# A hybrid decoder step on one core: five buffers for the decay rows, and the convolution half of the output projection ahead of the scan's half

## What is computed

```python
proj = rmsnorm(h) @ w_in                        # 1024 -> gate/value of a conv, z, x/B/C, dt
glu   = proj[:, :1024] * sigmoid(proj[:, 1024:2048])
a_out = silu(layernorm(causal_dwconv(glu)))     # 31 taps, 1024 channels: the "conv half"
xbc   = silu(causal_dwconv(proj[..., o2:o3]))   # 4 taps
y     = ssd_scan(x, dt, a_neg, B, C, state)     # 16 heads in 4 groups, chunks of 128
y     = (y + d_skip * x) * silu(z)
m_out = rmsnorm(y per group of 256)             # the "state half"
h = h + concat(a_out, m_out) @ w_out            # 2048 -> 1024
h = h + hier_moe(rmsnorm(h))                    # 16 experts, 2 of a token's group
h = h + (p @ w_ple) * sigmoid(rmsnorm(h) @ w_ple_gate)
return rmsnorm(h), and the new conv and scan states
```

## Time and profile before

| what | value |
|---|---|
| time, median of 3 runs (lowest to highest) | 586.15 us (583.11 to 587.26) |
| profiled execution: its time, its span | 586.09 us, 584.4 us |
| mean granted TensorE clock | 0.98 |
| busy: PE, DVE, ACT, POOL | 540.7, 265.1, 164.1, 85.2 us |
| HBM read, written | 155.06 MB, 8.84 MB |

### The profile page before, as it was taken

How to read it: one execution, slowest core, us unless ns; L and a number is a source line. 1 busy time by engine, 2 the same in 40 slices (tenths; PEclk the granted TensorE clock), 3 DMA queues, 4 the chain that set the end, 5 groups by cost and what they waited for, 6 DMA issues and landing times.

```text
span 584.4 us, 7620 instructions
## 1 busy us (share of the span) xinstructions
PE 540.7 (93%) x2749; PEld 351.1 (60%) x2749; DVE 265.1 (45%) x783; ACT 164.1 (28%) x386; POOL 85.2 (15%) x103
## 2 busy tenths in 40 slices
PE   5999999997896878999989899999999999999994
PEld 3788888885555657888764334343434343444882
DVE  0799798438447776102253032323232322323653
ACT  3211311116568783502242111111101010102433
POOL 4000063413425540030000000000000000000000
PEclk9999999999989879999989999999999999999997
DMA  8844443687956867793296996999999999999001
GB/s 339 270 145 146 144 145 144 169 238 234 253 181 202 296 232 315 296 370 152 93 384 259 421 422 270 382 423 422 421 423 421 421 422 420 423 419 422 33 0 74
DMA packets 35692, 164.27 MB, mean 281 GB/s; under 512 B 5768, under 2 KB 12744, under 8 KB 19664
## 3 DMA queue, kind: packets, MB, share of 16 engines
q1 hardware_dynamic: 25200, 140.27, 62.1%
q0 software_dynamic: 5920, 21.27, 10.3%
q10 hardware_dynamic: 4544, 2.37, 1.5%
HBM read 155.06 MB, written 8.84 MB: 280 GB/s over the span
## 4 chain that ended last, share of the span: by engine, by line
PE 86%; DVE 7%; issue 2%; DMA 2%; ACT 1%; POOL 1%; DVEq 0%; POOLq 0%; ACTq 0%
PE ps L968 21%; PE ps L1220 19%; PE ps L1067 10%; PE ps L1250 10%; PE ps L1195 5%; PE ps L1283 5%; PE ps L917 2%; DMA asg<-acs_rows 2%; PE ps L1122 2%; DVE xraw_s L1502 1%; PE ps L1153 1%; PE ps L935 1%; PE ps L1147 1%; PE ps L1160 1%; PE ps L959 1%
## 5 line engine op out<-in xcount | busy, mean ns | idle before, releaser
L968 PE MATMUL ps<-u,ring 128*128 128x264 f32 x640 | 145.6, 389 | 0.0
L968 PEld LDWEIGHTS ps<-u,ring 128*128 128x128 f32 x640 | 122.6, 192 | 22.0 <-issue 0.8
L1220 PE MATMUL ps<-ring,xraw 128*64 128x512 f32 x464 | 103.0, 595 | 5.0 <-DVE glu L1714 4.9
L1220 PEld LDWEIGHTS ps<-ring,xraw 128*64 128x64 f32 x464 | 33.9, 137 | 62.6 <-issue 61.1
L1250 PE MATMUL ps<-ring,xraw 128*64 128x512 f32 x256 | 58.5, 598 | 0.7 <-ACT xraw L880 0.7
L1067 PE MATMUL ps<-cat,ring 128*128 128x264 f32 x256 | 57.6, 387 | 1.6 <-DVE cat L1552 1.6
L1067 PEld LDWEIGHTS ps<-cat,ring 128*128 128x128 f32 x256 | 48.5, 190 | 10.6 <-issue 2.4
L632 POOL DMA_INDIRECT xbc<-u_rows,slot_tok x8 | 7.6, 952 | 258.0 <-DVE slot_tok L1669 258.0
L1250 PEld LDWEIGHTS ps<-ring,xraw 128*64 128x64 f32 x256 | 16.9, 136 | 32.1 <-issue 28.8
L558 POOL TENSOR_TENSOR glu<-asg 128x256 f32<-128x256 f32 x8 | 21.4, 2673 | 96.3 <-ACT asg L704 96.3
L1714 DVE COPY glu<-ps 128x264 f32<-128x264 f32 x8 | 3.5, 433 | 68.2 <-PE ps L1260 68.2
(11 more groups left out here) (299 smaller groups left out, 631.8 us busy)
## 6 DMA issues: line engine op xcount, KB each, us to landing
ring<-in_w_moe SPq DMA_DIRECT2D x90, 1024.0 KB, 14.4
ring<-in_w_in SPq DMA_DIRECT2D x20, 1024.0 KB, 5.2
ring<-in_w_out SPq DMA_DIRECT2D x8, 1024.0 KB, 6.1
ring<-in_state_s POOLq DMA_DIRECT2D x8, 512.0 KB, 9.7
out_h_s_out<-ring POOLq DMA_DIRECT2D x8, 512.0 KB, 5.7
ring<-in_w_pleg SPq DMA_DIRECT2D x4, 1024.0 KB, 23.2
asg<-acs_rows ACTq DMA_DIRECT2D x8, 256.0 KB, 6.4
glu<-bc_rows POOLq DMA_DIRECT2D x4, 512.0 KB, 6.4
```

What stands on the lines that cost most here:

```text
L968: ins = mm(ps[:, BANK[n], 0:T], wv[:, k, q * P:(q + 1) * P], u[:, k, :], start=(k == 0), stop=(k == KD - 1))
L1220: ins = mm(ps[e * CAP:(e + 1) * CAP, gu, :], xg[:, 4 * hf + k, e * CAP:(e + 1) * CAP], wk, start=(hf == 0 and k == 0), stop=(hf == 1 and k ...
```

## The change

Two parts. First, `acs` gets five buffers instead of two (`NACS`): two where they were, three in `hs_all`, which is free once its rows have been turned; the three further spreads are issued right behind the first two, and later ones as buffers come free. Second, the order of the two halves of the output projection is exchanged. The layer norm's two means move into TensorE's scan loop (behind items 3 and 5), its subtraction, root, products and Silu into the loops of VectorE and ScalarE (items 4, 6 and 7). The conv half comes first, in banks 0, 1, 2 and 7, and VectorE adds its blocks to `h` one at a time (`add_a`); the state half follows and is added separately. ScalarE does the state `decode` of tiles 0 to 3 in the scan and of 4 to 7 behind it; VectorE does 0 to 2 in the scan. SP's table puts each `load_first` two weight loads later, and w_out's halves are taken in the other order.

```diff
-        acs = asg[:, :, :, :].rearrange("p a b n -> p (a b n)")[:, 0:8 * Q].rearrange("p (q r n) -> p q r n", q=2, r=4)
+        acs_of = lambda x, q: [x.rearrange("p a n -> p (a n)")[:, 4 * Q * i:4 * Q * i + 4 * Q].rearrange("p (r n) -> p r n", r=4)
+                               for i in range(q)]
+        acs = acs_of(asg[:, :, :, :].rearrange("p a b n -> p (a b) n"), 2) + acs_of(hs_all[:, :, :], 3)
+        AB = [0, 1, 2, 7]
 # SP
-                    sp.wait_ge(out_used, n - NWIN + 1)
+                    sp.wait_ge(a_psum, 2 * (n - NWIN) + 2)
-                src = w_in[n] if n < NWIN else w_out[n - NWIN]
+                src = w_in[n] if n < NWIN else w_out[(n - NWIN + NWOUT // 2) % NWOUT]
-                for j in {22: (0, 1, 2, 3), 23: (4, 5), 24: (6, 7), 25: (8,)}.get(n, ()):
+                for j in {24: (0, 1, 2, 3), 25: (4, 5), 26: (6, 7), 27: (8,)}.get(n, ()):
                     load_first(j)
 # GpSimd
-            pool.wait_ge(ln_n, 4)
 # ScalarE
             spread(0)
             spread(1)
+            act.wait_ge(htok_psum, 1)
+            for i in range(2, NACS):
+                spread(i)
...
+                if i == NG:
+                    act.wait_ge(ln_xc, 1)
+                    a.activation(ln_sqr, cat[:, 0:8, :], ACT.Square).then_inc(ln_sq, 1)
                 if i == 6:
+                    act.wait_ge(ln_stat, 2)
+                    link(a.activation(ps[:, 7, 0:T], ps[:, 7, 0:T], ACT.Ln, bias=eps[:, 0:1]))
+                    a.activation(ps[:, 7, 0:T], ps[:, 7, 0:T], ACT.Exp, scale=-0.5).then_inc(g_root, 1)
                     act.wait_ge(proj_evac, Z_SILU)
                     z0 = zs[:, 0:6, :]
                     a.activation(z0, z0, ACT.Silu)
-                decode(i)
+                if i == 7:
+                    for j in range(KD):
+                        act.wait_ge(ln_n, j // 2 + 1)
+                        a.activation(cat[:, j, :], cat[:, j, :], ACT.Silu, scale=par("ln_g", j), bias=par("ln_b", j))\
+                            .then_inc(a_out_ready, 1)
+                if i % 2:
+                    decode(i // 2)
...
             load_table(ACT.Ln)
+            decode(4)
+            decode(5)
+            square_y(0)
+            decode(6)
+            decode(7)
+            for gr in range(1, NG):
+                square_y(gr)
 # TensorE
                 item(i)
+                if i == 3:
+                    ...
+                    mean_of(cat, 7, mean_k).then_inc(ln_stat, 1)
+                if i == 5:
+                    pe.wait_ge(ln_sq, 1)
+                    mean_of(ln_sqr, 7, mean_k).then_inc(ln_stat, 1)
...
+            pe.wait_ge(proj_evac, NSEQ)
+            pe.wait_ge(xtok_ready, 4)
             for n in range(KD):
-                if n == KD - 1:
-                    pe.wait_ge(ln_n, 4)
-                w_out_half(n, 0)
-                if n == 2:
-                    pe.wait_ge(ln_sq, 1)
-                    mean_of(glu, 7, mean_k).then_inc(ln_stat, 1)
+                if n >= 4:
+                    pe.wait_ge(a_added, n - 3)
+                w_out_half(n, 0).then_inc(a_psum, 1)
+                if n == 3:
+                    pe.wait_ge(y_ready, 2 * NG)
+                    pe.wait_ge(st_ready, 2 * NG)
+                    pe.wait_ge(btok_ready, 2)
+                    group_mean(0)
+                if n == 6:
+                    for gr in range(1, NG):
+                        group_mean(gr)
 # VectorE
+                if i == NG:
+                    dve.wait_ge(ln_stat, 1)
+                    v.tensor_tensor(cat[:, 0:8, :], ...subtract).then_inc(ln_xc, 1)
                 take(i)
...
-                if i >= 2:
-                    decode(i - 2)
+                if i == 6:
+                    dve.wait_ge(g_root, 1)
+                    for j in range(0, KD, 2):
+                        v.tensor_tensor(cat[:, j:j + 2, :], ...mult).then_inc(ln_n, 1)
+                if i in (3, 5, 7):
+                    decode((i - 3) // 2)
...
+            def add_a(n):
+                dve.wait_ge(a_psum, n + 1)
+                v.tensor_tensor(h[:, n, :], h[:, n, :], ps[:, AB[n % 4], 0:T], ALU.add).then_inc(a_added, 1)
...
-            for gr in range(3):
-                gate_y(gr)
+            gate_y(0)
+            decode(3)
+            gate_y(1)
+            add_a(0)
+            decode(4)
+            add_a(1)
+            decode(5)
+            gate_y(2)
+            add_a(2)
             decode(6)
+            add_a(3)
             decode(7)
             gate_y(3)
```

More of the change, by code:

```diff
@@ L30 @@
 NPR = 256
+NACS = 5
 NSM = 8
@@ L131, in build @@
         x4 = scratch[:, 4096:6200].rearrange("p (q i t) -> p q i t", q=2, i=4)
-        outer = [scratch[:, at:at + 1024].rearrange("p (b n) -> p b n", b=NSM) for at in (8192, 9216, 6200)]
+        outer = [scratch[:, at:at + 1024].rearrange("p (b n) -> p b n", b=NSM) for at in (8192, 9216, 6208)]
+        ln_sqr = scratch[:, 4096:4096 + KD * T].rearrange("p (j n) -> p j n", j=KD)
         glu_s = scratch[:, 10240:12224].rearrange("p (j k b) -> p j k b", j=KD, k=KC)
@@ L286, in build @@
         rows_stored = sem("rows_stored")
-        acs_loaded = [sem(f"acs_loaded{q}") for q in range(2)]
+        acs_loaded = [sem(f"acs_loaded{q}") for q in range(2)] + in_x + [in_small]
+        NACS_BASE = [0, 0, 16, 16, 48]
         b_loaded = [sem(f"b_loaded{q}") for q in range(2)]
@@ L788, in _ @@
             exp_of(0)
-            spread(2)
             evacuate(NFIRST + 1)
@@ L802, in _, with square_y @@
                     a.activation(z0, z0, ACT.Silu)
-                decode(i)
+                if i == 7:
[5 more added lines that the diff above has]
+                    decode(i // 2)
                 for n in AFTER_ITEM[i]:
                     evacuate(n)
-            load_table(ACT.Ln)
-            for gr in range(NG):
+            def square_y(gr):
                 act.wait_ge(ycat_ready, gr + 1)
@@ L819, in _ @@
                 a.activation(o, o, ACT.Exp, scale=-0.5).then_inc(g_root, 1)
-            act.wait_ge(ln_xc, 1)
-            act.wait_ge(out_conf, 32)
-            a.activation(glu[:, :, 0:T], cat[:, 0:8, :], ACT.Square).then_inc(ln_sq, 1)
-            act.wait_ge(ln_stat, 2)
-            link(a.activation(ps[:, 7, 0:T], ps[:, 7, 0:T], ACT.Ln, bias=eps[:, 0:1]))
-            a.activation(ps[:, 7, 0:T], ps[:, 7, 0:T], ACT.Exp, scale=-0.5).then_inc(g_root, 1)
-            load_table(ACT.Silu)
-            for j in range(KD):
-                act.wait_ge(ln_n, j // 2 + 1)
-                a.activation(cat[:, j, :], cat[:, j, :], ACT.Silu, scale=par("ln_g", j), bias=par("ln_b", j))\
-                    .then_inc(a_out_ready, 1)
             load_table(ACT.Ln)
@@ L1041, in _, with group_mean @@
                 item(i)
+                if i == 3:
+                    pe.wait_ge(conv_done, KD - len(PE_CONV))
+                    pe.wait_ge(conv_s_done, 1)
+                    pe.wait_ge(proj_evac, POS["c", 7, 0] + 1)
+                    pe.wait_ge(btok_ready, 1)
+                    mean_of(cat, 7, mean_k).then_inc(ln_stat, 1)
+                if i == 5:
+                    pe.wait_ge(ln_sq, 1)
+                    mean_of(ln_sqr, 7, mean_k).then_inc(ln_stat, 1)
                 for n in AFTER_ITEM[i]:
                     project(n)
-            pe.wait_ge(conv_done, KD - len(PE_CONV))
-            pe.wait_ge(proj_evac, NSEQ)
-            pe.wait_ge(conv_s_done, 1)
-            pe.wait_ge(ea_ready, NG)
-            pe.wait_ge(dif_ready, 2 * NG)
-            mean_of(cat, 7, mean_k).then_inc(ln_stat, 1)
-            pe.wait_ge(rows_kept, 1)
-            pe.wait_ge(y_ready, 2 * NG)
-            pe.wait_ge(st_ready, 2 * NG)
-            for gr in range(NG):
+            def group_mean(gr):
                 pe.wait_ge(gsq_ready, gr + 1)
@@ L1553, in _ @@
                                            in1=ps[:, 3 + gr, 0:T], op0=ALU.mult, op1=ALU.mult).then_inc(m_out_ready, 1)
-            dve.wait_ge(g_root, NG + 1)
-            for j in range(0, KD, 2):
-                v.tensor_tensor(cat[:, j:j + 2, :], cat[:, j:j + 2, :],
-                                ps[:, 7, 0:T].unsqueeze(1).to_broadcast([P, 2, T]), ALU.mult).then_inc(ln_n, 1)
+            add_a(7)
+            dve.wait_ge(a_added, KD)
             def add_square(i, x, c):
```

48 lines of the change are left out of this document (27 added, 21 removed).

## The result

| | before | after |
|---|---|---|
| median (lowest to highest) | 584.98 us (581.04 to 587.26) | 589.26 us (586.44 to 592.44) |
| profiled execution: time, span | 586.09 us, 584.4 us | 590.0 us, 588.3 us |
| end of the output projection in it | 287.46 | 292.70 |

The medians are of 15 runs each, taken side by side. The ratio is 1.0068 (95% interval 1.0044 to 1.0093). The change is slower by 0.7%; 581.2 us had been predicted, within 575.5 to 588. The time lies above that range, and on the other side of the kernel before.

A forecast was written before the change was run, and what follows sets the result against it. TensorE was taken to bound the kernel (86% of the chain), but transfers to set the projection's new end: 287.5 - 282.6 = 4.9 us won, from 586.09 profiled (586.15 median) to 581.2 us, range 575.5 to 588.

The forecast's parts named there:

- The scan: TensorE's scan items: the second starts at 157.4, then 37.5 us back to back, so item seven ends at 194.9.
- ScalarE's chain: Between scan and projection, ScalarE sets the pace with 16.7 us of work; the convolution half starts at 211.6.
- The table loads: ScalarE's three table loads, two of them added, at 1.28 us each; rival of longer drain: 585.0 us, chance 0.08.
- The rate of full stretches: Ten weight and expert transfers at 421 GB/s take 24.9 us; at 358 GB/s, 29.3 us and a gain of 0.5.
- so the fourth block lands at 245.3 + 24.9 + 3.1 + 2.2 = 275.5; its two column blocks, 7.1, end at 282.6: State half's last weight block: last store, ten transfers, GpSimd's loads, landing extra, then matmuls; 4.9 us won.
- the chain of the prediction: State updates behind the scan, decays, GpSimd adds and reloads in series: last add at 239.3, last store in at 245.3.
- mostly under the transfers: Lower clock after TensorE's holes at 237 and before the second block: nothing to 1.7 us each, mostly covered by transfers.
- The state chain slips: Rival: two serial state reloads take 9.7 us each, last store lands at 254.5, 590.4 us; chance 0.13.
- TensorE idles here: In the projection, conv blocks last until 237.4, the last group mean until 243.9; TensorE idles between.
- the rows still come late: Rival at the scan's start: item two still starts at 160.16, 2.8 us later, 584.0 us; chance 0.10.

The follow-up runs named there:

- e3: Changed kernel with separate semaphores for stores of even and odd state tiles, so GpSimd no longer waits for its own last store; 587.55 us, ratio 1.0034 to before.
- e1: Changed kernel with all nine early expert tiles behind the last w_out load in SP's list; 578.55 us, ratio 0.9867 to before.
- e11: Changed kernel with five state decays in the scan instead of four, three behind it, nothing else; 582.16 us, ratio 0.9948 to before.
- e6: Changed kernel with the edits of both e1 and e3; 577.31 us, ratio 0.9869 to before.
- e4: Kernel before with five row buffers alone, halves not exchanged; 577.55 us, ratio 0.9873 to before.
- e10: e6 with five state decays in the scan instead of four, three behind it; 570.71 us, ratio 0.9748 to before.
- e7: Changed kernel with one expert tile instead of four ahead of the state half's second weight block, five then ahead of the third; 589.2 us, ratio 1.0035 to before.
- e2: Changed kernel with GpSimd's 1.3 MB of loads (pT, w_ple) held back behind the first four finished blocks; 585.31 us, ratio 0.9996 to before.
- e12: e10 with VectorE masking the last item ahead of the layer norm's products; 567.41 us, ratio 0.9702 to before.

## Why the prediction was wrong

**What held.** The scan: second item at 157.71 (157.4 predicted), item seven through at some 195.7 (194.9). ScalarE's chain: the conv half at 211.88 (211.6), though the last item and projection were covered by only half a microsecond (through at 210.94, ScalarE at 211.46). The table loads cost the 1.28 us that their rows show. The Trainium skill's page "ScalarE: Activation LUTs", section "What ACT_TABLE_LOAD costs", has 1.38 us of drain on top of each switch. The rows at 196.35 to 199.80 have no room for it. The rate of full stretches is 421 to 424 GB/s again (the two stretches above; the earlier trace rows, read to its end, has 419 to 423). The Trainium skill's page "DMA: Bandwidth & Descriptors", section "Bandwidth", has about 358 as the limit of the HBM side, as the prediction says, but also 425 measured on a single core with the pair's other core idle. This case agrees with the second. That a transfer and not TensorE alone would set the end was right too, but it was another block's.

**The step that failed: "so the fourth block lands at 245.3 + 24.9 + 3.1 + 2.2 = 275.5; its two column blocks, 7.1, end at 282.6".** The landing was summed too short, and it was held against TensorE at the last block only. The fourth block landed at 283.3 (24.4 us after its issue at 258.89), 7.8 us later than the sum says, and held nothing up: TensorE came to its two column blocks only at 285.30. What held TensorE up was the second block. It is wanted first, with six column blocks, about 22 us, still to do behind it. By the prediction's own figures it would land at 245.3 + 4 x 2.49 + 3.1 + 2.2 = 260.6 and also give an end of 282.6: there was no slack at either place, so comparing both would have shown the risk, but not another time. It landed at 268.19, 7.6 us later:
- 1.5 us: the last store was in at 246.83 instead of 245.3 (the prediction's own 239.3 + 5.7 make 245.0). The last add was 4.2 late. Of that, 2.9 are GpSimd's wait for its own store, by e3; the chain of the prediction left this wait out. The store itself took 3.01 instead of 5.7.
- 2.5 us, the share of one tile: four tiles stood ahead, not three. The first waits for the last state product, and that ended at 245.55 (241.3 predicted).
- about 3.6 us are left: traffic that the sum left out (2.01 MB of GpSimd's in that stretch, not 1.3) and the rate. 8.23 MB in 22 us is 374 GB/s, not 421. How these two share the 3.6 us was not measured.

From the landing to the end it then took 24.5 us instead of 22.0. Of these 2.5 us, 2.0 are the lower clock behind the wait (16.46 us for 64 records instead of 14.51), which the prediction had put "mostly under the transfers". 7.6 + 2.5 make the 10.1 us between 282.6 and 292.70. In e1, with the tiles out of the way, 9.9 of them are gone.

**The rival that came near.** "The state chain slips" gave 590.4 us, and 589.26 was measured, but that is chance: it needed a last store later than 250.2, and the store was in at 246.83. In e11 it goes out 8.5 us sooner and TensorE waits 7.39; in e1 it goes out at 243.04, about as in the change, and there is no wait. The order of the queue decides whether there is a wait, not the store.

**What the prediction had not seen at all** is that the exchange could gain little even with its loads in order: e6 ends the projection at 281.51, e4 with the old order at 282.70. Of the 9.7 us by which e6 starts it sooner, 1.2 are left at the end: 6.3 us go into holes ahead of the group means, and the rest mostly into slower records behind the holes (the last mean and the 112 records behind it take 2.05 and 25.92 us in e6; 112 records take 25.08 in e10). Each order has 16 records of means inside the projection, so the means themselves cost no more than before. The holes are there because the change had put four of eight state decays behind the scan: e10 has three there, closes the holes and gains 7 us. The prediction did show the idle time ("TensorE idles here") and let it pass, since transfers were to end last anyway.

**Five buffers** were priced at 2.8 us in the rival "the rows still come late"; they are worth 3.3 in the changed kernel, and some 7 in the old one, where the slow convolution behind the hole (5.35 us at 161.38) was in the trace and was not counted.

## What to carry to other kernels

When a load is put behind others in one queue, check the landing of every block against the moment that block is wanted, not just the last: bytes ahead of it in the queue, beside it in others, and the work still left behind it. Where a change frees an early start, follow the longest chain that it pushes back (here four state decays) to its end before the gain is counted. And price a hole of TensorE with the slow matmuls that may follow it.

## What the runs showed of the hardware

A megabyte's landing time says little without its place in the queue: the same kind of weight block landed 18.57 us after its issue as the fifth in SP's queue, and the eight of e1, with no tile ahead of them, 4.8 to 8.3 us after it. The Trainium skill, page "DMA: Bandwidth & Descriptors", section "Queues, rings and completion order", says that descriptors of a ring are consumed in its order and that the engines take turns between queues by packets; e7 agrees with the first: behind one tile instead of four, the second block landed 10.0 us after its issue. e2 agrees with the second: without GpSimd's 1.3 MB beside it, it landed 3.1 us sooner after its issue.

Issuing a load sooner does not land it as much sooner: the load of state 7 took 5.42 us from 230.81, 7.83 from 225.52 and 9.31 from 225.73, the last two while a weight block and the stores were on their way. That these slowed it was not tested by itself.

Not each hole of TensorE is followed by the lower clock. Behind 9.47 us it came (0.88 granted from 270 to 280, 16.46 us for 64 records), behind 4.81 us too (0.70 us for a row that takes 0.45 elsewhere), and behind 2.78 us in the kernel before (5.35 us for a convolution that takes 3.67 elsewhere). Behind 2.72 us in e12 it did not (14.51 us for 64 records, as after 0.48). So the length of the hole alone does not tell.
